# Twenty projection tiles of a hybrid layer as ten couples by seven block products

## The reference

```
proj = jnp.einsum("bld,de->ble", x, w_in)
q, k, v, z_attn, z_ssm, xbc, dt_raw = jnp.split(proj, IN_SPLITS, axis=-1)
attn = sliding_window_attention(q, k, v, sinks) * jax.nn.silu(z_attn)
xbc = jax.nn.silu(causal_depthwise_conv(xbc, conv_w, conv_b))
```

## Time and profile before

| | us |
|---|---|
| median of three runs | 3050.71 |
| lowest, highest | 3045.12, 3054.69 |
| the profiled execution | 3048.31 |
| its span from first to last instruction | 3045.7 |
| of it TensorE busy | 2909.7 |

### The profile page before, as it was taken

The page is one execution under the profiler, slowest core; times in us unless marked ns, Lnnn a source line. Parts: engine busy times, 40 slices in busy tenths (PEclk is TensorE's granted clock), DMA queues, the critical chain, the costliest instruction groups (busy, mean ns, idle before and its releaser), DMA issues. The chain is left out here.

```text
span 3045.7 us, 50150 instructions
## 1 busy us (share of the span) xinstructions
PE 2909.7 (96%) x20830; PEld 2306.3 (76%) x20830; DVE 1747.6 (57%) x2684; ACT 1264.3 (42%) x2255; POOL 963.7 (32%) x596
## 2 busy tenths in 40 slices
PE   6999788899999999999999999999999999999998
PEld 4888278777788887887877777777878777777776
DVE  4999855557655558872233543488522434435885
ACT  3010433353444444451244444675322344446753
POOL 3443012214655550002333333143133333332421
PEclk8999799999999999999999999999999999999999
DMA  5111600031222226223112313675431122137754
GB/s 223 51 49 28 235 4 4 18 139 56 83 83 83 83 77 255 80 106 113 50 49 76 89 46 102 222 258 191 156 96 53 49 77 84 49 97 264 251 173 149
DMA packets 291392, 331.41 MB, mean 109 GB/s; under 512 B 12224, under 2 KB 235840, under 8 KB 286688
## 3 DMA queue, kind: packets, MB, share of 16 engines
q1 hardware_dynamic: 223936, 267.27, 26.8%
q10 hardware_dynamic: 67232, 60.96, 6.3%
HBM read 260.95 MB, written 65.14 MB: 107 GB/s over the span
## 5 line engine op out<-in xcount | busy, mean ns | idle before, releaser
L2849 PE MATMUL PS<-x_high_sb,w_high_sb 128*128 128x512 f32 x1296 | 519.3, 401 | 0.0
L2849 PE MATMUL PS<-x_low_sb,w_high_sb 128*128 128x512 f32 x1296 | 506.0, 390 | 0.0
L2849 PE MATMUL PS<-x_high_sb,w_low_sb 128*128 128x512 f32 x1296 | 505.2, 390 | 0.0
L2849 PEld LDWEIGHTS PS<-x_high_sb,w_high_sb 128*128 128x128 f32 x1296 | 243.3, 188 | 71.4 <-issue 23.9
L3101 DVE CUSTOM_DVE_ANT_0 scores_sb<-PS,attn_raw_sb,sinks_sb 128x256 f32<-128x256 f32 (+1 forms) x256 | 104.4, 463 | 334.4 <-PE PS L2867 334.4
L2849 PEld LDWEIGHTS PS<-x_high_sb,w_low_sb 128*128 128x128 f32 x1296 | 243.3, 188 | 53.1
L2849 PEld LDWEIGHTS PS<-x_low_sb,w_high_sb 128*128 128x128 f32 x1296 | 243.7, 188 | 46.6
L2952 POOL CAST w_high_sb<-xbc_sb 128x1024 fp32r<-128x1024 f32 x80 | 82.9, 1037 | 502.6 <-PE PS L2849 488.6
L3347 PE MATMUL PS<-w_high_sb,attn_high_sb 128*128 128x512 f32 x512 | 218.0, 426 | 13.1 <-DVE attn_low_sb L3640 10.9
L2030 PE MATMUL PS<-h_high_sb,up_parts_sb 128*128 128x512 f32 x640 | 204.2, 390 | 2.6 <-DVE up_parts_sb L2106 1.8
L3053 ACT COPY probs_turned_sb<-PS 128x512 f32<-128x512 f32 x56 | 32.8, 586 | 409.7 <-PE PS L2882 409.7
(11 more groups left out here) (540 smaller groups left out, 6159.6 us busy)
## 6 DMA issues: line engine op xcount, KB each, us to landing
xbc_sb<-w_in SPq DMA_DIRECT2D x80, 512.0 KB, 3.7
ada_slots_sb<-ada_w SPq DMA_DIRECT2D x16, 1024.0 KB, 6.3
decays_sb<-running_sums SPq DMA_DIRECT2D x16, 1024.0 KB, 7.8
attn_raw_sb<-state_out ACTq DMA_DIRECT2D x32, 512.0 KB, 3.6
attn_raw_sb<-attn ACTq DMA_DIRECT2D x28, 512.0 KB, 6.2
wo_raw_sb<-w_up SPq DMA_DIRECT2D x24, 512.0 KB, 4.9
xbc<-staged_sb ACTq DMA_DIRECT2D x24, 512.0 KB, 3.2
xbc_sb<-xbc SPq DMA_DIRECT2D x16, 768.0 KB, 6.6
```

What stands on the lines that cost most here:

```text
L2849: last = pe.matmul(PS[:, bank, :], a[:, n % 2, k], b[:, k, cols], start=k == 0 and a is WH and b is HH, stop=k == KT - 1 and a is WL)
```

## The change

The 41 tiles of a layer are dealt out anew:

- Three plain tiles (dt, zs0, zs1) come first, while x is turned and its sums are made.
- Twenty tiles (v, q0, q1, za0, za1, the twelve xbc, k) become ten couples of two tiles in a new function and code block, `paired_projections`. A couple is a product of 2 x 2 blocks (two column tiles; 512 rows of the inner dimension; 512 tokens), computed by seven block products A11, A12, S1 to S4 and A22, of 12 matmuls each. S1 to S4 need sums of weight blocks (GpSimd, for each couple) and sums of x blocks T1 to T4 (VectorE, once for each layer, with high parts by ScalarE). Partial results are copied out of PSUM by ScalarE (`snap`) and joined by VectorE (`join`). v, q0, q1, za0, za1, k and dt are stored to memory and loaded again by the next code block.
- Two plain tiles, q2 and q3, begin at the end of that block (`next_parts`); q3, za2 and za3 come at the start of the next one.
- Fourteen tiles (the other q, za and zs) stand beside attention, seven of their 224 steps of three matmuls beside each unit.
- VectorE takes `gate` of unit u-1 before `inverse` of unit u. GpSimd scales the probabilities as before.

The weights that a layer finds loaded ahead are now those of dt. The core of the diff, shortened:

```diff
+COVER = [("dt", 0), ("zs", 0), ("zs", 1)]
+COUPLES = [("v", 0), ("q", 0), ("za", 0)] + [("xbc", 2 * i) for i in range(XT // 2)] + [("k", 0)]
+NEXT = [("q", 2), ("q", 3)]
+def couple_order(n_last):
+    order = [(0, "A11"), (0, "A12")]
+    for n in range(n_last + 1):
+        if n:
+            order += [(n, "A11"), (n - 1, "S4")]
+        order += [(n, "S2"), (n, "S1"), (n, "S3")]
+        if n < n_last:
+            order += [(n + 1, "A12"), (n, "A22")]
+    return order + [(n_last, "A22"), (n_last, "S4")]
...
+        bank_of = lambda n, kind: 4 * (n % 2) + {"A12": 0, "S1": 1, "S4": 1}.get(kind, 2)
+        result = lambda n, c: bank2(m, 2 * (n % 2) + c)
...
+                elif kind == "A12":
+                    if n == 1:
+                        pe.wait_ge(s.act_free, 3)
+                    elif n > 1:
+                        bank_free(pe, n - 2, 0)
+                elif kind == "S2":
+                    pe.wait_ge(s.snap, snap_at[n, "1"])
+                    pe.wait_ge(s.tlo, HK)
...
+                elif kind == "A22":
+                    if n == last:
+                        pe.wait_ge(s.next_split, 1)
+                        bank_free(pe, last - 1, 0)
+                        half_tile(next_parts, 0, 0)
+                    pe.wait_ge(s.joined, join_at[n, "22"])
...
+            x.scalar(act)
+            act.wait_ge(src_stored, 16 * TT)
+            cover(0)
+            act.wait_ge(x.s.turned, 2 * KT - x.ahead)
+            turned_high("2", lambda k: HK + 2 * k + 2)
+            turned_high("1", lambda k: HK + 2 * k + 1)
+            cast(0, "A11")
+            cast(0, "A12")
+            cast(0, "S2")
+            cover(1)
+            turned_high("3", lambda k: 3 * HK + 2 * k + 2)
+            cast(0, "S1")
+            cast(0, "S3")
+            turned_high("4", lambda k: 5 * HK + 2 * k + 2)
+            cover(2)
+            for n in range(last + 1):
+                if n:
+                    evacuate(n - 1, 1)
+                    cast(n, "S1")
+                    cast(n, "S3")
+                snap(n, "1")
+                if n < last:
+                    cast(n + 1, "A12")
+                cast(n, "A22")
+                if n:
+                    evacuate(n - 1, 0)
+                    finish(n - 1, 1)
+                snap(n, "V")
+                snap(n, "5")
+                if n < last:
+                    cast(n + 1, "A11")
+                cast(n, "S4")
+                if n:
+                    finish(n - 1, 0)
+                if n < last:
+                    cast(n + 1, "S2")
...
+            for n in range(last + 1):
+                if n:
+                    taps(n - 1, 1)
+                    join(n - 1, "12")
+                low(n, "A22")
+                if n < last:
+                    low(n + 1, "A11")
+                if n:
+                    taps(n - 1, 0)
+                join(n, "11")
+                low(n, "S4")
+                join(n, "22")
+            join(last, "12")
...
+                mine = steps[PER * u:PER * (u + 1)]
                 if u:
                     turn(u - 1)
-                half_tile(F + u, 0)
+                for at in mine[:3]:
+                    product(*at)
                 if u:
                     out(u - 1)
-                half_tile(F + u, 1)
+                for at in mine[3:5]:
+                    product(*at)
                 if u + 1 < N:
                     scores(u + 1)
+                for at in mine[5:]:
+                    product(*at)
```

More of the change, by code:

```diff
@@ L2747, in projections_and_attention @@
         lo = lambda nb: P if nb == 0 else 0
-        first = [("k", 0), ("k", 1), ("v", 0), ("v", 1), ("dt", 0), ("q", 0), ("q", 1), ("za", 0), ("za", 1)]
-        rest = [("xbc", i) for i in range(XT)] + [("zs", i) for i in range(KT)]
-        beside = []
-        for g in range(KVH):
-            ahead = [] if g == KVH - 1 else [("q", 2 * g + 2), ("q", 2 * g + 3), ("za", 2 * g + 2), ("za", 2 * g + 3)]
-            beside += ahead + rest[:TT - len(ahead)]
-            rest = rest[TT - len(ahead):]
+        first = [("q", 2), ("q", 3), ("za", 2), ("za", 3)]
+        beside = [("zs", 2), ("zs", 3)] + [(kind, 2 * g + i) for g in (2, 3) for kind in ("q", "za") for i in range(2)]
+        beside += [("zs", i) for i in range(4, KT)]
         jobs = first + beside
@@ L2801, in first_weights @@
+            sp.dma_start(KH[0:HD, 2:4], k_swapped[HD:P]).then_inc(s.heads_in, 16)
+            sp.dma_start(KH[HD:P, 2:4], k_swapped[0:HD]).then_inc(s.heads_in, 16)
+            kept(("q", 0), QT[:, 0:2], s.heads_in)
+            weights(4)
+            kept(("za", 0), AT[:, 0:2], s.za_in)
+            biases(1)
+            for n in range(5, len(jobs)):
+                weights(n)
+                if n in (12, 15):
+                    biases(2 if n == 12 else 3)
             def first_weights(i):
@@ L2808, in _ @@
             first_weights(2)
-            for i in range(2):
-                sp.wait_ge(stage[i], 16 * sum(slot[j] == i for j in staged if j[0] == "xbc"))
-            sp.wait_ge(s.split, len(jobs))
+            sp.wait_ge(s.split, len(jobs) - 2)
             for c in range(2):
@@ L2862, in scores @@
                 if nb == 0:
-                    free(pe, where["q", 2 * g + 1])
+                    if g:
+                        free(pe, where["q", 2 * g + 1])
+                    else:
+                        pe.wait_ge(s.heads_in, 64)
                 for i in range(G4):
@@ new lines, in _ @@
+            half_tile(1, 0)
+            half_tile(1, 1)
+            free(pe, 0)
+            pe.wait_ge(s.v_in, 16)
+            for l in range(TT):
+                for c in range(2):
+                    last = pe.transpose(PS[:, l // 2, (l % 2) * KVW + c * P:(l % 2) * KVW + (c + 1) * P],
+                                        ST[:, c, l * P:(l + 1) * P], m.const("ident"))
+            last.then_inc(s.small, 1)
+            half_tile(2, 0)
+            pe.wait_ge(s.dt_in, 16)
+            pe.wait_ge(s.small_free, 1)
@@ L2925, in _ @@
+            for l in range(TT):
+                last = pe.transpose(PS[:, l // 4, (l % 4) * P:(l % 4 + 1) * P], dt_at[:, l * P:(l + 1) * P],
+                                    m.const("ident"))
+            last.then_inc(s.small, 1)
+            half_tile(2, 1)
+            half_tile(3, 0)
+            pe.wait_ge(s.small_free, 2)
+            step.tensor_sums(pe)
+            half_tile(3, 1)
             step.tensor_ends(pe)
-            pe.wait_ge(s.swapped, 32)
             scores(0)
             for u in range(N):
+                mine = steps[PER * u:PER * (u + 1)]
@@ L3037, in exps @@
+                    free(act, n)
+                    store((kind, i))
             def exps(u):
@@ L3153, in _ @@
                     move1(u - 1)
+                    gate(u - 1)
                 if u < N:
                     inverse(u)
-                if u:
-                    taps(F + u - 1)
-                    gate(u - 1)
-    gates_stored = [(stage[i], 16 * sum(slot[j] == i for j in staged if j[0] in ("xbc", "zs"))) for i in range(2)]
-    return gates_stored
+    return first_stored + [(stage[i], 16 * sum(slot[j] == i for j in gates)) for i in range(2)]
 def state_space_and_mix(m, layer, d_skip, xbc_d, gate_d, rows_d, attn_d, y_d, src, w, ln_g, ln_b, dst, ahead,
```

685 lines of the change are left out of this document (507 added, 178 removed).

## The result

| | before | after |
|---|---|---|
| median, us | 3047.97 (4 runs) | 3105.02 (4 runs) |
| lowest to highest | 3045.12 to 3054.69 | 3096.32 to 3108.79 |
| span of the profiled execution | 3045.7 | 3100.5 |

The ratio is 1.018, with a 95% interval from 1.015 to 1.021. The change makes the kernel 57 us slower, clear of the scatter, although TensorE has 240 matmuls fewer.

What follows compares the result with a forecast made beforehand. TensorE, busy 96% of the span, was taken as the bound, so each new wait costs its full length. Added waits of 55 us per layer, 110 in two, less 54.4 gained, gave +55.4: median 3106 us, range 3065 to 3140.

Steps and rivals of the forecast that it cites:

- The gain: Ten couples save 120 matmuls per layer, 240 in two, at 0.2267 us each: 54.4 us.
- Term 1: Middle of the couples: five TensorE waits per layer on VectorE's late taps, 3.4 us plus 1.7 clock each, 25 us.
- Term 2: Opening, per layer: first tile ends 5 us later, first S2 stalls 8 us with clock; 1.3 more for clock steps.
- Term 3: End of the couples: TensorE waits 3.9 us for GpSimd's split of q2, plus 1.7 clock, 5.6 us per layer.
- Term 4: A further code block: crossing of 1.9 us idleness and perhaps a clock step, 3 us per layer.
- Term 5: Attention beside 14 tiles: GpSimd's splits delay TensorE's output 0.5 us in 12 units, 1 at the start, 7 us per layer.
- Rival A: The stalls come but TensorE's clock holds, so every clock addition goes: 3078 us; chance 0.16.
- The reading that the fall is paid once a stage: Skill page's reading of the clock: term 1 would be 5 x 3.4 = 17 plus one 1.7.
- Rival B: Couples run covered: taps done within S3's 2.7 us, against a 6.1 us chain, so term 1 is zero; faster, chance 0.08.
- rival C: Everything but term 1 comes as forecast: 3056 us, no difference; chance 0.06.
- Rival D: Attention becomes a chain, its unit taking 9.0 us rather than 7.9: 3176 us; chance 0.10.

Runs made afterwards that it cites:

- e11_quiet: e7 plus the stores of e9, the early casts of e10, and GpSimd's three sums for couple 1 held back until VectorE finished T4: 3028.7 us, ratio 0.9928.
- e1: Changed kernel with VectorE's taps of couple n-1 moved ahead of the low part of A11 of couple n+1: 3055.2 us, ratio 1.0015.
- e2: Changed kernel with ScalarE's cast of A11 of couple n+1 moved ahead of the copy of S1 of couple n: 3064.3 us, ratio 1.0045.
- e3: Changed kernel with ScalarE's third cover tile and first couple's copies of A11 and S2 ahead of the last T4 conversions: 3085.1 us, ratio 1.0108.
- e7: Changed kernel with e1, e3, e4, and VectorE's low parts of x's last four blocks ahead of their subtractions: 3036.7 us, ratio 0.9959.
- e10: Changed kernel with e1, e3, e4, the stores of e9, and ScalarE's first-couple casts of A12 and A22 ahead of T4's conversions: 3038.9 us, ratio 0.9962.
- e4: Changed kernel with GpSimd's split of the first plain tile after the couples waiting for S1 of the last couple, not S3: 3100.0 us, ratio 1.0157.
- e9: e7 with the last two stores of attention's output issued by SyncE rather than ScalarE: 3036.6 us, ratio 0.9958.
- e8: e7 with VectorE's inverse ahead of the gate again in the attention units: 3037.2 us, ratio 0.9957.

## Why the prediction was right

It said 3106 us and slower; it is 3105. The mechanism was right: new waits of TensorE, at the places named, that cost more than the removed matmuls gave. The sum is near in its parts, per layer, in us:

| term | predicted | layer 0 | layer 1 | from |
|---|---|---|---|---|
| 1. taps in the couples | 25 | 24.0 | 25.0 | 5 x (23.90 - 19.10), 5 x (24.10 - 19.10) |
| 2. first cover tile | 5 + 1.3 | 6.0 | 4.9 | ScalarE takes up the second tile |
| 2. first S2 | 8 | 9.5 | 10.4 | wait 7.5, and 36 slower matmuls |
| 3. the plain tile | 5.6 | 6.7 | 6.8 | 3.69 and 19.66 - 0.32 - 72 x 0.2267 |
| 4. further code block | 3 | 1.7 | 1.7 | 0.32, and 3.36 - 1.95 |
| 5. attention | 7 | 2.9 | 2.9 | 31 x (8.06 - 7.97) |
| not foreseen: step sizes | 0 | 0 | 1.7 | wait at L2712 |
| sum | 55 | 50.8 | 53.4 | added cost measured: 52.5, 55.1 |

A unit took 8.06 us from turn to turn and 14.09 before, which less 27 matmuls at 0.2267 is the 7.97. Some 1.7 us in each layer are in no row of the table. That the time came within 1 us is in part luck: the forecast was 4 us too high for attention and 1 to 2.4 too low for the first S2 and for the plain tile, in each layer, and the measured added cost is 107.6 us where 110 was said.

- **The gain** of 54.4 us is there as work: 20590 matmuls in place of 20830. With most of the waits taken out (e11_quiet) the two stages are 30.5 us shorter than before; 23.9 us of added cost are left.
- **Term 1.** The chain stands in the trace as it was worked out: 3.18 us of wait where 3.4 was said, ten times, at the places named. e1 and e2 show its cause. The clock was put at 1.7 us; it took (23.90 - 19.10) - 3.18 = 1.6.
- **Term 2.** The first tile ended 4.2 us later, relative to the start of the stretch; behind it a short wait and, in layer 0, slow matmuls made that 6.0. For the first S2 the wait was 7.5 where 6.5 was said, and the clock took 2 to 2.8 us, not 1.7. It waited for what the prediction said, ScalarE's copy behind T4. What was not seen is that most of the work behind this wait is due soon after: e3 could take only 6.0 and 8.3 us of it away, and e7 and e10 nothing more, until GpSimd was held back.
- **Term 3.** The wait (3.9 said, 3.7 measured) was right, and a detail of its reason wrong: the parts of q2 lie in the places of S1 and A11, only those of q3 in that of S3. That made it cheap to mend (e4). The clock took 3.0 us here where 1.7 was said; two windows of 3 us behind the wait, in the changed kernel, stand below this list.
- **Term 4** was in the wrong place. The crossing into attention costs 0.32 us; the one out of it grew from 1.95 to 3.36, since ScalarE ends last (e9).
- **Term 5** was too high. GpSimd's split does hold VectorE's tiny operation (1.99 us in one unit), but the copy behind it made TensorE wait 0.18 us at most, not 0.5, three times in layer 0 and twice in layer 1, not in 12 units. Most of the 2.9 us comes from the new order of TensorE itself, which the prediction didn't count. The tile matmuls of a unit stand in three runs now, two before, and in each run the second starts 0.33 us after the first, the later ones 0.23 apart (rows below the list). That is 30 more times 0.10 us in a layer, 3.1. Against it the turns took 1.7 us less in a layer; no run was made on either, and why a run starts so is open.
- **The clock.** Rival A, that it holds, is refuted for the gaps of 3.2, 3.7 and 7.5 us, and true for those of 1.1 (e2) and 1.5 us (e4). Length is not all: in the first cover tile of layer 0 four gaps of 0.3 to 1.0 us follow each other, and the clock fell behind them too (0.56, the window below the list), where in layer 1, with fewer of them in this place, it stayed at 1.00. The reading that the fall is paid once a stage, which the prediction set beside the Trainium skill's page "TensorE: Matmul & The Clock Gate", section "What's actually happening", would have given 17 + 1.7 in term 1; 24.0 and 25.0 were measured, and the granted clock was at 0.50 behind such a wait (first window of e2_cast). That reading was too narrow: the section's table of the two states has the slow clock come back after idleness too, and with that the trace agrees.
- Rival B's point (6.1 against 2.7 us) is what e1 moves. With term 1 gone and the others left its kernel came out at 3055.2 us, which is rival C's 3056. Rival D, the chain of attention, is refuted by e8 and by units of 8.06 us.

A run of tile matmuls in a unit of attention (term 5), first, second and third:

```profile
1729.71 0.50 PE L3371 MATMUL PS<-x_high_sb,w_high_sb 128*128 128x512 f32 x1
1730.05 0.40 PE L3371 MATMUL PS<-x_low_sb,w_high_sb 128*128 128x512 f32 x1
1730.28 0.40 PE L3371 MATMUL PS<-x_high_sb,w_low_sb 128*128 128x512 f32 x1
```

The window behind the four short gaps in layer 0's first cover tile:

```profile
1409.00:1412.00 3.00, 3.00 (x8) 2.39 (x9) 1.11 (x1) 2.52 (x5) 2.92 (x2) 0.56 0.43 175
```

The windows for term 3, with 7 and 9 matmuls in 3 us each at a granted clock of 0.50 and 0.53, and the one behind the wait of 1.52 us in e4_split, with 13 at 1.00:

```profile
1655.00:1658.00 3.00, 2.96 (x7) 2.42 (x8) 0.00 (x0) 0.00 (x0) 2.92 (x2) 0.50 0.00 0
1658.00:1661.00 3.00, 3.00 (x9) 2.28 (x9) 0.00 (x0) 0.00 (x0) 0.36 (x1) 0.53 0.00 0
```

```profile
1654.30:1657.30 3.00, 2.98 (x13) 2.51 (x14) 0.00 (x0) 0.00 (x0) 2.92 (x2) 1.00 0.17 49
```

## What to carry to other kernels

Fewer instructions on the engine that bounds a kernel pay only if the helpers bring every operand in time, so read their order for an instruction that has its input but stands behind one that waits: here that cost 50 us, and two lines moved gave it back. Where VectorE bounds a stretch on SBUF tiles, hold back what GpSimd can do later, and after each wait removed ask which operand is late next. An edit of a few microseconds is judged by the stretch of the trace that it changes, since the rest of this program varied by 16 us between executions.

## What the hardware showed that was not expected

- A wait costs more than its length when TensorE's clock falls behind it: 3.18 us cost 4.8 to 5.0, 3.69 us cost 6.7, while 1.07 us cost 1.3 and 1.52 us cost 1.8 (16.96 - 0.32 - 72 x 0.2267 = 0.3 behind it).
- Four gaps of 0.77, 0.96, 0.96 and 0.32 us, with three matmuls between each two, were followed by a granted clock of 0.56; a single gap of 1.52 us was followed by 1.00.
- GpSimd is slowed as well: its subtraction of 2.34 us took 2.89 beside one VectorE operation of 0.69.
- The crossing between two code blocks cost TensorE 0.32 us where it was the last to finish, and 3.36 where ScalarE was.
- Behind a switch from small matmuls to those of a tile, the second tile matmul starts 0.33 us after the first instead of 0.23, so work cut into more runs costs TensorE time without any wait.
